# A chunked gated-delta layer: the 64x64 triangular inverse built from 32x32 blocks

## The reference, cut to what matters

```python
kb = kc * bc[..., None]
n_mat = jnp.where(strict, -jnp.einsum('nbhid,nbhjd->nbhij', kb, kc) * decay, 0.0)
t_mat = jnp.eye(CHUNK, dtype=f32) + n_mat
p_mat = n_mat
for _ in range(int(math.log2(CHUNK)) - 1):
    p_mat = jnp.einsum('nbhij,nbhjk->nbhik', p_mat, p_mat)
    t_mat = t_mat + jnp.einsum('nbhij,nbhjk->nbhik', t_mat, p_mat)
u = jnp.einsum('nbhij,nbhjd->nbhid', t_mat, vb)
w = jnp.einsum('nbhij,nbhjd->nbhid', t_mat, kb * jnp.exp(gc)[..., None])
```

## Time and profile before

| | us |
|---|---|
| median of 3 runs | 2711.65 (2710.69 to 2711.97) |
| the profiled execution, its own time | 2707.76 |
| its span, first to last instruction | 2706.0 |
| PE busy | 2682.5 (99%) |
| DVE busy | 1416.5 (52%) |
| ACT busy | 971.0 (36%) |
| POOL busy | 398.7 (15%) |

### The profile page before, as it was taken

The page is one execution under the profiler, slowest core; times in us unless marked ns, Lnnn a source line. Parts: engine busy times, 40 slices in busy tenths (PEclk is TensorE's granted clock), DMA queues, the critical chain, the costliest instruction groups (busy, mean ns, idle before and its releaser), DMA issues.

```text
span 2706.0 us, 50329 instructions
## 1 busy us (share of the span) xinstructions
PE 2682.5 (99%) x19808; PEld 2274.0 (84%) x19808; DVE 1416.5 (52%) x3633; ACT 971.0 (36%) x3158; POOL 398.7 (15%) x238
## 2 busy tenths in 40 slices
PE   7999999999999999999999999999999999999998
PEld 6888888888888888888888888888888888888887
DVE  6777777233366666612236666651224666665012
ACT  4555455422244444421124444442112444444101
POOL 4333333443100110000000110000000011000000
PEclk9999999999999999999999999999999999999999
DMA  7554554787733333255453333335546333333564
GB/s 249 201 180 167 182 193 170 264 288 279 253 121 111 128 128 117 107 203 217 172 219 130 112 114 125 130 110 203 216 172 220 113 118 128 123 112 125 183 222 171
DMA packets 79001, 458.43 MB, mean 169 GB/s; under 512 B 13232, under 2 KB 17456, under 8 KB 31792
## 3 DMA queue, kind: packets, MB, share of 16 engines
q1 hardware_dynamic: 65664, 427.85, 44.2%
q10 hardware_dynamic: 13104, 27.36, 3.0%
HBM read 352.42 MB, written 102.76 MB: 168 GB/s over the span
## 4 chain that ended last, share of the span: by engine, by line
PE 96%; DMA 2%; POOL 1%; DVE 1%; ACT 0%; issue 0%; POOLq 0%; SPq 0%; ACTq 0%; DVEq 0%
PE bank L1305 24%; PE bank L1307 23%; PE bank L1306 23%; PE bank L1450 2%; PE last_banks L1450 2%; PE last_banks L1415 2%; PE bank L1434 2%; PE last_banks L1434 2%; PE bank L1403 2%; PE bank L1499 1%; PE bank L1491 1%; PE bank L1475 1%; PE last_banks L1557 1%; PE bank L1483 1%; PE bank L1548 1%; PE bank L1538 1%
## 5 line engine op out<-in xcount | busy, mean ns | idle before, releaser
L1305 PE MATMUL bank<-hT_hi,w_sl 128*128 128x512 f32 x2112 | 872.8, 413 | 0.0
L1307 PE MATMUL bank<-hT_hi,w_sl 128*128 128x512 f32 x2112 | 827.3, 392 | 0.0
L1306 PE MATMUL bank<-hT_lo,w_sl 128*128 128x512 f32 x2112 | 825.5, 391 | 0.0
L1307 PEld LDWEIGHTS bank<-hT_hi,w_sl 128*128 128x128 f32 x2112 | 396.7, 188 | 86.1
L1305 PEld LDWEIGHTS bank<-hT_hi,w_sl 128*128 128x128 f32 x2112 | 398.3, 189 | 71.6 <-issue 0.7
L1306 PEld LDWEIGHTS bank<-hT_lo,w_sl 128*128 128x128 f32 x2112 | 398.8, 189 | 65.4 <-issue 0.7
L436 POOL TENSOR_TENSOR w_sl<-w_raw,w_sl 128x1024 fp32r<-128x1024 f32 x90 | 218.3, 2430 | 391.2 <-ACT w_sl L517 381.6
L982 DVE SCALAR_TENSOR_TENSOR area<-zraw,stc,area 128x512 f32<-128x512 f32 x288 | 220.2, 765 | 4.2
L1148 DVE SCALAR_TENSOR_TENSOR s_cur<-s_cur,scs,last_banks 128x128 f32<-128x128 f32 x112 | 38.9, 348 | 199.8 <-PE last_banks L1554 199.8
L611 ACT ACTIVATE area<-area 128x512 f32<-128x512 f32 x96 | 60.4, 629 | 219.6 <-DVE area L982 219.6
L455 POOL TENSOR_TENSOR gu<-mk,g_hi 128x512 fp32r<-128x512 f32 x32 | 41.9, 1309 | 643.7 <-DVE nmx L1102 603.8
(11 more groups left out here) (244 smaller groups left out, 4817.7 us busy)
## 6 DMA issues: line engine op xcount, KB each, us to landing
w_sl<-saved_w SPq DMA_DIRECT2D x270, 1024.0 KB, 4.8
saved_w<-w_sl SPq DMA_DIRECT2D x90, 1024.0 KB, 4.9
w_raw<-in_w_tiles SPq DMA_DIRECT2D x90, 512.0 KB, 5.9
area<-in_x ACTq DMA_DIRECT2D x4, 2048.0 KB, 10.4
area<-in_x ACTq DMA_DIRECT2D x14, 512.0 KB, 8.1
out_y<-area ACTq DMA_DIRECT2D x3, 2048.0 KB, 8.1
bias_sb<-in_bias ACTq DMA_DIRECT2D x32, 128.0 KB, 2.3
out_y<-area SPq DMA_DIRECT2D x4, 512.0 KB, 2.7
```

The source lines that it names most:

```text
L1305: pe.matmul(dst, a_hi, b_hi, start=first, stop=False)
L1306: pe.matmul(dst, a_hi, b_lo, start=False, stop=False)
L1307: return pe.matmul(dst, a_lo, b_hi, start=False, stop=last)
```

## The change

Everything below is float32, as before.

- The levels work on 32x32 blocks, four to a tile, all 16 blocks of the head in one go and in one bank (bank 6). There are 4 levels with powers 2 to 16 and one last step with the projection alone. `square` is gone: one matmul per block, with P^T as weights, gives the next power and the projection side by side (32, 64, 64, 64 and 32 columns).
- The weights of the next level need the power transposed. DVE does that with a 32x32 block transpose (`dve.transpose`) straight from bank 6, after ACT has copied the untransposed power from the same bank. For the last level ACT's copy falls away.
- The transpose of F on TensorE stays, but ACT copies only its coupling part (`od`). The first transposed power comes from DVE (`first_powers`).
- Two 32x32 blocks make a 64x64 one with two products (`inner_in`, `inner_out`) ahead of the old merge; ACT copies the first (`yt`), DVE the second (`inner_corners`).
- On TensorE, `fill(11)` ahead of the levels becomes `fill(8)`, one step follows each level and `inner_in`, `fill(2)` ahead of `merge_in` goes, `probs(0)` moves behind the first level, and `logits_quarters` moves as a whole to just before `merge_in`.
- Once at the start, DVE makes `stacked`, a 128x32 tile with the four 32x32 identities.

```diff
+        BLOCKS = tuple(slice(r, r + BL) for r in range(0, P, BL))
+        CORNERS = ((BLOCKS[0], BLOCKS[1]), (BLOCKS[2], BLOCKS[3]))
+        f_blk, u_blk, fu_blk, p_blk = ptt[:, :, 0:BL], ptt[:, :, BL:2 * BL], ptt[:, :, 0:2 * BL], ptt[:, :, 2 * BL:3 * BL]
...
@@ ScalarE, head
-                for lo, hi in HALVES:
-                    ins = act.activation(ptt[lo:hi, :, 0:CH], tt[lo:hi, :, lo:hi], ACT.Copy)
+                for r in BLOCKS:
+                    ins = act.activation(f_blk[r], tt[r, :, r], ACT.Copy)
                 ins.then_inc(pt0_ready, 1)
...
+                def power_copy(l):
+                    act.wait_ge(powers_done, powers(n1, l))
+                    act.activation(f_blk, bch(6)[:, :, 0:BL], ACT.Copy).then_inc(power_copied, 1)
+
                 softmax_exp(0)
+                power_copy(1)
                 probs_copy(0)
-                for l in range(1, LEVELS + 1):
-                    p_copy(l, 0)
-                    p_copy(l, 1)
+                for l in range(2, LEVELS):
+                    power_copy(l)
                 fill(1)
...
@@ VectorE, head
+                def first_powers():
+                    dve.wait_ge(pt0_ready, n1)
+                    dve.transpose(p_blk, f_blk)
+                    dve.tensor_tensor(u_blk, f_blk, stacked[:, None, :].to_broadcast([P, NT, BL]), ALU.add).then_inc(powers_ready, 1)
...
+                def level(l):
+                    dve.wait_ge(powers_done, powers(n1, l))
                     if l < LEVELS:
+                        dve.wait_ge(power_copied, (n1 - 1) * (LEVELS - 1) + l)
+                    ins = dve.transpose(p_blk, bch(6)[:, :, 0:BL])
                     if l > 1:
+                        dve.wait_ge(powers_ready, powers(n1, l))
+                        ins = dve.tensor_tensor(u_blk, bch(6)[:, :, BL:2 * BL], u_blk, ALU.add)
+                    ins.then_inc(powers_ready, 1)
...
                 def diagonal():
+                    dve.wait_ge(powers_ready, powers(n1, LEVELS + 1))
+                    dve.wait_ge(powers_done, powers(n1, LEVELS + 1))
+                    ch.link(dve.tensor_tensor(u_blk, bch(6)[:, :, BL:2 * BL], u_blk, ALU.add))
+                    dve.transpose(vt, u_blk).then_inc(merge_dve, 1)
+                    for r in BLOCKS:
+                        ins = copy(tt[r, :, r], u_blk[r])
                     ins.then_inc(diag_ready, 1)
...
                 logits(0)
+                first_powers()
                 attention()
                 fill(1)
                 quotient(0)
-                fill(2)
-                dve.wait_ge(tt0_ready, n1)
-                for l in range(1, LEVELS + 1):
-                    level(l, 0)
-                    level(l, 1)
-                settled()
+                fill(1)
+                level(1)
+                fill(1)
+                for l in range(2, LEVELS + 1):
+                    level(l)
                 diagonal()
+                inner_corners()
...
@@ TensorE, head
+                def apply(l):
+
+                    c0, c1 = (0 if l <= LEVELS else BL), (2 * BL if l > 1 else BL)
+                    pe.wait_ge(powers_ready, powers(n1, l))
+                    for t in range(NT):
+                        for r in BLOCKS:
+                            ins = pe.matmul(bch(6)[r, t, c0:c1], p_blk[r, t, :], fu_blk[r, t, c0:c1], start=True, stop=True)
+                    ins.then_inc(powers_done, 1)
+
+                def inner_in():
...
+                            ins = pe.matmul(bch(5)[c, t, 0:BL], tt[a, t, c], vt[a, t, :], start=True, stop=True)
+                    ins.then_inc(merge_product, 1)
+
+                def inner_out():
...
+                            ins = pe.matmul(bch(7)[a, t, 0:BL], yt[c, t, :], u_blk[c, t, :], start=True, stop=True)
+                    ins.then_inc(merge_product, 1)
...
-                fill(11)
-                probs(0)
-                for l in range(1, LEVELS + 1):
-                    square(l, 0)
-                    apply(l, 0)
-                    square(l, 1)
-                    apply(l, 1)
+                fill(8)
+                for l in range(1, LEVELS + 2):
+                    apply(l)
+                    fill(1)
                     if l == 1:
-                        logits_quarters(0)
-                logits_quarters(1)
-                apply(LEVELS + 1, 0)
-                apply(LEVELS + 1, 1)
-                fill(2)
+                        probs(0)
+                inner_in()
+                fill(1)
+                inner_out()
+                logits_quarters()
                 merge_in()
```

More of the change, by code:

```diff
@@ L21 @@
 NEG = -3.0e38
[L22 to L23 removed]
+BL = 32
+LEVELS = 4
 HEAD_TILES = 6
@@ L89, in state_steps, with powers, merges @@
     return (n1 - 1) * NT + t + 1 - max(0, n1 - 1 - (NB - 1) * H)
+def powers(n1, l):
+    return (n1 - 1) * (LEVELS + 1) + l
+def merges(n1, step):
+    return (n1 - 1) * 3 + step
 class Chain:
@@ L147, in build_program @@
         mk = sb("mk", [P, 5, P])
+        stacked = sb("stacked", [P, BL])
         after_r = sb("after_r", [P, P], F32R)
@@ L1060, in level @@
                     if l > 1:
-                        if l > 2:
-                            dve.wait_ge(tt_ready[g], (n1 - 1) * (LEVELS - 1) + l - 2)
-                        c0 = first_column(l)
-                        dve.tensor_tensor(ptt[:, PAIR[g], c0:P], a[:, PAIR[g], c0:P], ptt[:, PAIR[g], c0:P], ALU.add).then_inc(tt_ready[g], 1)
-                def settled():
-                    for g in range(2):
-                        dve.wait_ge(tt_ready[g], n1 * (LEVELS - 1))
-                        for lo, hi in HALVES:
-                            ins = copy(tt[lo:hi, PAIR[g], lo:hi], ptt[lo:hi, PAIR[g], CH:P])
-                    ch.inc(ins)
@@ L1083, in corner, with inner_corners @@
+                def inner_corners():
+                    dve.wait_ge(merge_product, merges(n1, 2))
+                    for a, c in CORNERS:
+                        ins = copy(tt[a, :, c], bch(7)[a, :, 0:BL])
+                    ins.then_inc(merge_dve, 1)
                 def corner():
@@ L1419, in head @@
                 fill(7)
-                def square(l, g):
-                    width = CH if l < LEVELS else CH - LAST
-                    if l == 1:
-                        pe.wait_ge(p0_ready, n1)
-                        pe.wait_ge(pt0_ready, n1)
-                        pe.wait_ge(attn_ready, n1)
-                    else:
-                        pe.wait_ge(p_ready[g], n5 + l - 1)
-                        pe.wait_ge(pt_ready[g], (n1 - 1) * (LEVELS - 1) + l - 1)
-                    for t in (2 * g, 2 * g + 1):
-                        for lo, hi in HALVES:
-                            ins = pe.matmul(pv(bank[P_BANK[g]])[lo:hi, t, 0:width], ptt[lo:hi, t, 0:CH], p_sb[(l - 1) % 2][lo:hi, t, 0:width], start=True, stop=True)
-                    ins.then_inc(p_done[g], 1)
@@ L1476, in logits_padded, with logits_quarters @@
                     ins.then_inc(lg_done[0], 1)
-                def logits_quarters(g):
+                def logits_quarters():
                     pe.wait_ge(prob_ready[0], n1)
-                    for t in (2 * g, 2 * g + 1):
+                    for t in range(NT):
                         c = (NT + t) * CH
```

100 lines of the change are left out of this document (33 added, 67 removed).

## The result

The changed kernel takes 2649.0 us (median of four, 2648.8 to 2649.18) against 2711.17 beside it: a ratio of 0.977, interval 0.975 to 0.979. The forecast was 2651. The profiled execution took 2649.18 us with a span of 2647.4, so 58.6 less than the 2707.76 of before.

What follows compares the result with a forecast made beforehand. TensorE's own issue was taken as the bound: 7.64 us of work plus 0.38 of waits, 8.02 against 9.89 a head, saves 1.87, 60 us in 32 heads, giving a median of 2651 us; range 2636 to 2690.

Steps and rivals of the forecast that it cites:

- Groups of four: TensorE's level products: four blocks run side by side, 0.058 us a group with 64 columns, 0.032 with 32.
- Rival 1: Narrow weights bring nothing (0.058 us a group) or transposes are somewhat slow (0.5 us): 2678 us; chance 0.15.
- rival 2: Only two row groups go side by side: 2711 us; all four queue for one bank: 2834; chance 0.06 in all.
- Ways out and back: TensorE between projection and small tiles: 0.14 us in, 0.22 back, 0.36 each; five more times a head give back 1.8.
- The transpose: DVE's transpose between levels: takes 0.29 us like a copy, and the next DVE instruction starts 0.21 after it.
- Rival 3: DVE's transpose is slow: at 0.8 us the gain is used up, at 1.0 the kernel takes 2740; chance 0.07.
- The waits between levels: Levels 2 to 3 and 3 to 4: chain 1.24 us over ACT and DVE, cover 1.05, so 0.38 a head.
- The sum of a head: Levels to merge on TensorE, waits included: 8.02 us against 9.89, so 1.87 saved a head.
- The timeline of one head serves for all 32: Premise: every head has the same instructions in the same order, so one head's terms were taken for 32.
- 1.1 us of slack: At `probs`: DVE's 1/sum is ready 1.1 us before TensorE wants it, despite the earlier start of the levels.
- 7 + 8 + 6 + 2 ahead of the state steps where there were 22: Projection steps of a head: their number stays 48, only their places differ.

Runs made afterwards that it cites:

- dve_copies: Changed kernel with DVE instead of ACT copying each new power ahead of its transpose; 2640.21 us, ratio 0.974.
- pool_in_levels: Changed kernel with one GpSimd weight subtraction moved behind the norm factors, all held until the previous head's output is split or level 3 is ready; 2638.12 us.
- pool_pieces: Changed kernel with GpSimd's subtraction for the low part of a weight tile issued as four pieces of 256 columns; 2663.46 us, ratio 0.983.
- rsqrt_first: Changed kernel with one of the two GpSimd weight subtractions ahead of a head's norm factors moved behind them; 2650.87 us, ratio 0.9786.

## Why the prediction was right

- **Groups of four.** Forecast 0.058 (64 columns) and 0.032 (32 columns) a group; measured 0.056 by doubling and 0.032 from start to start, 0.038 by doubling. Rival 1 (0.058 whatever it holds) and rival 2 (two at a time, or a queue) fall. Four row groups do go side by side in one bank; the queue that rival 2 weighed is not there.
- **Ways out and back.** Forecast 0.36 each. The stretch of level 1, 0.71 less 0.227, plus 0.126, is 0.61; forecast 0.62. `probs` and level 2: 1.34 becomes 1.24 against 1.26. The last one, with quarters, merge and values: 2.94 becomes 2.84 against 2.88.
- **The transpose.** Forecast 0.29 with the next instruction 0.21 behind; measured 0.317 and 0.24. Rival 3 falls: it would have needed 0.8.
- **The waits between levels.** Forecast chain 1.24, cover 1.05, wait 0.19 twice. The trace has 1.23 and two waits of 0.17. The single hops were off both ways (ACT starts 0.06 behind the matmuls' end, ACT to DVE is 0.10 instead of 0.04, DVE to TensorE 0.06 instead of 0.15) and cancel: luck in the parts, not in the kind of chain. `dve_copies` shows the mechanism: a chain 0.17 shorter, and both waits are gone. That PE's list of waits would name them was wrong.
- **The sum of a head.** Forecast 1.87 saved. The later blocks save 2.15; the new stretches add up to 7.84 us against 8.02, and the remaining 0.1 lies outside them.
- **What failed.** "The timeline of one head serves for all 32: in every head the same instructions stand in the same order." The order is the same, but the head was one of the second block, where GpSimd doesn't subtract. In the first block DVE's small instructions are held for up to 2.3 us ahead of `F` and of `probs`, and TensorE came right behind DVE even before the change. So "1.1 us of slack" at `probs` is right for the later blocks (1.3 measured) and wrong for the first, where 0.65 are missing. The step that moved ahead of the state steps ("7 + 8 + 6 + 2 ahead of the state steps where there were 22") was counted, but not what it had covered: `F`, now 0.72 late.
- **Luck in the total.** Eight heads at 1.87 would have saved 15 us in the first block; it saves 6.6, 8.4 less. The later blocks save 52.3 where 24 heads at 1.87 make 44.9, 7.4 more. The two errors nearly cancel, and the sum lands within 2 us of the forecast. `pool_in_levels` gives back 11.9 us of the first block.

## What to carry to other kernels

Where cover is taken from a place, look at its slack in every phase of the program, not in one head: the same code stood under a different load in the first quarter. An engine that starts a fixed 0.15 us behind another one's end, head after head, has no slack there, even where the list of waits is silent. Small products between large ones cost little themselves, and what they cost is the chain from level to level; a copy moved onto the engine that needs it next can be cheaper than one beside it on another engine. And background work of GpSimd did least harm here beside DVE instructions that read PSUM.

## What the runs showed of the hardware

- Sixteen f32 products of 32x32 tiles in four row groups and one bank: four start within 0.02 us, and the next four 0.032 (32 columns) or 0.056 us (64 columns) later. That is 0.008 us for a record with 32 columns. The Trainium skill (TensorEngine Tiling (Array Packing), Gotcha 1) says that different row tiles cannot access the same PSUM bank simultaneously. The measured pace shows no such queue: four records with 64 columns in one bank take 0.056 us together, as long as a pair on 64x64 tiles did.
- A TENSOR_SCALAR or SCALAR_TENSOR_TENSOR of DVE on 128x4 elements in SBUF takes 0.165 us alone and up to 2.35 while GpSimd subtracts 128x1024, and a TENSOR_TENSOR on 128x512 with two inputs in SBUF 2.75 instead of 0.69. DVE instructions with an operand in PSUM keep their duration (the addition 0.25, the transpose 0.32). So do two that work in SBUF alone: the 32x32 block transpose (L1070, 0.31 in the 8 cases beside a subtraction and in the other 24) and, in `pool_pieces`, RECIPROCAL on 128x4 (0.18 in 9 cases beside a piece and in the other 55).
- The holding goes both ways: in `pool_pieces` a piece of GpSimd's subtraction takes 0.73 us, and 1.18 beside DVE's products on 128x512 elements with two inputs in SBUF.
- A run of small matmuls can have gaps for which the profile names no engine: 16 of up to 2.8 us with 352 records a head; with 192 none in the changed kernel and one of 1.0 in `rsqrt_first`; one of 0.3 in the kernel before. What brings them about stays open.
